# Gathering the tokens of two pairs of experts at once, and using three weight units in 24 unsplit instead of two, in a mixture-of-experts stage on one core

## The chip, the cores and the metric

The kernel runs on one core of one Trainium2 chip (trn2). The metric is device time in microseconds (us) from the start to the end of one launch. TensorE is written PE in the rows (PEld for its weight loads), VectorE is DVE, ScalarE is ACT, GpSimd is POOL, and SyncE (SP) issues nearly all DMA.

## What is computed

A one-layer transformer trunk in float32 over 256 tokens of width 2048: two token mixers (latent attention and retention), a gated merge, and then a hierarchical mixture of experts. The change touches the experts alone:

```python
def hier_moe(h, w_group, b_group, w_expert, b_expert, w1, w3, w2):
    ...
    g_sel = jnp.argmax(g_logits + b_group.astype(jnp.float32), axis=-1)
    ...
    _, e_local = lax.top_k(e_logits + e_bias, TOP_K)
    e_w = jax.nn.softmax(jnp.take_along_axis(e_logits, e_local, axis=-1), axis=-1) * g_prob[:, None]
    ...
    y = grouped_expert_ffn(xf, e_id, w1, w3, w2)
    out = jnp.einsum('nkd,nk->nd', y.reshape(n_tok, TOP_K, d), e_w.astype(y.dtype))
```

There are 32 experts, two are chosen for each token, and each expert is `(silu(x @ w1) * (x @ w3)) @ w2` with `w1` and `w3` of 2048 x 512 and `w2` of 512 x 2048.

## The kernel before

The first part of the launch (to about 1100 us) is the mixers. The change leaves it alone. Then comes the expert stage, which reads all 32 experts' weights once: 384 **units** of 1 MB, each a `[128, 2048]` tile of float32. An expert has 12 units, four each of `w1`, `w3` and `w2`. Experts are worked in 16 **pairs**, pair 0 to pair 15, with 24 units a pair. A unit has a place x in its pair from -4 to 19, and its step is k = x + 4. The steps of pair p are: k 0 to 3 `w1` of expert 2p, 4 to 7 `w2` of expert 2p-1, 8 to 11 `w3` of 2p, 12 to 15 `w1` of 2p+1, 16 to 19 `w2` of 2p, 20 to 23 `w3` of 2p+1. Pair 0 has no k 4 to 7, and four last `w2` units follow pair 15.

**One unit.** SyncE loads it into a ring of 8 slots (`raw2`; four early units have places of their own, `raw_e`). The load into a slot waits until TensorE is done with the unit that lay there 8 units before. ScalarE copies the unit to a rounded form (`hi`, line 636, tile `wh2`, 4 slots, so it waits until TensorE is done with the unit 4 before). VectorE subtracts it from the raw one (`lo`, line 786, written in place as `wl2`). TensorE then runs 8 matmuls of 512 columns, one on `wh2` and one on `wl2` for each quarter (lines 1119 and 1120). Such a unit is **split**. A unit that is **whole** (the places in `XR`, and the very first unit) is used by TensorE from the raw tile in plain float32 (line 1116) without work of ScalarE or VectorE: 4 matmuls in the program, shown by the trace as 8 of about 0.43 us.

**Gather.** Each expert has 64 slots for tokens. The tokens of a pair are gathered by TensorE: VectorE makes a 0/1 matrix `pg` (line 843), TensorE multiplies it with the token tiles `xh1` and `xl1` (the rounded part and the rest), 128 columns at a time (`gather`, line 1089, 8 calls of 8 matmuls a pair, one call behind each of the steps in `G_AT` = 4, 6, 8, 10, 16, 18, 20, 22 of the pair before), into PSUM banks 7 and 6 in turn. ScalarE copies each bank to `xg` (line 641). `xg` holds two pairs.

**Between.** `mix` (lines 1141 and 1144, 20 entries in the trace) transposes an expert's up-projections behind k 0 and k 12, into banks 6 and 7 too. Then come the sigmoid on ScalarE (653) and the product on VectorE (914 to 927, `hidden`). The outputs are scaled and added at k 7 and k 19 (ScalarE 660, VectorE 951). GpSimd scatters them to DRAM. In pair 15 ScalarE also copies the tokens of the second tile (line 707, steps 1 and 10), which the final sum takes. Each engine runs its instructions in the order written, and semaphores join the engines.

**The end.** Behind the last units SyncE reads the scattered rows back (`yrow`), TensorE adds the stream and the last pair, and VectorE normalises and the result goes out.

## Time and profile before

| | us |
|---|---|
| median of 3 runs | 2134.16 |
| lowest and highest | 2133.64, 2135.18 |
| span of the profiled execution | 2134.4 |
| TensorE busy | 2069.4 (97%) |
| TensorE weight loads | 1749.8 (82%) |
| VectorE busy | 1592.3 (75%) |
| ScalarE busy | 1286.2 (60%) |
| moved by DMA | 606.48 MB, 284 GB/s over the span |

The profiled execution is known by its span alone, from the first to the last instruction. Busy shares are averages over both parts of the launch, so the rows below are taken from the expert stage. Matmuls overlap in the trace, so the time of one is its start-to-start distance, not its listed duration.

### The profile page before, as it was taken

The page shows a single profiled execution, that of the slowest core. Times are in us where ns is not written, and L with a number is a line of the kernel's source. Part 1 is how long each engine was busy: PE and PEld are TensorE (multiplying, and loading weights), DVE is VectorE, ACT ScalarE, POOL GpSimd, SP SyncE. Part 2 cuts the span into 40 slices and gives each one's busy share as a digit, 9 for nine tenths or more (in the row PEclk, how much of TensorE's full clock was granted, in tenths as well). Part 3 has the DMA queues.
Part 4 walks back from the last instruction along what each step waited for, and adds up shares of the span by engine and source line. Part 5 has one row for each costly group of instructions (what it writes and reads, how often), then busy time and mean ns, then how long its engine had stood idle before and what let it go on. Part 6 is the DMA issues. An engine that isn't in the chain of part 4 may idle for free.

```text
span 2134.4 us, 30028 instructions
## 1 busy us (share of the span) xinstructions
PE 2069.4 (97%) x11452; PEld 1749.8 (82%) x11452; DVE 1592.3 (75%) x1450; ACT 1286.2 (60%) x1064; POOL 104.7 (5%) x76
## 2 busy tenths in 40 slices
PE   8999999999999999999999999999999999999986
PEld 8998888899999998887887777777777787777764
DVE  7646664453646375455669999999999999999988
ACT  5445653333333323334347888888888888888883
POOL 1000000000000000001000000000000000000010
PEclk9999999999999999999999999999999999999998
DMA  6554335655454544557777999999999999999996
GB/s 215 159 139 158 118 120 186 208 180 172 146 176 148 166 157 143 192 197 239 233 297 287 399 421 421 421 420 419 418 420 418 421 418 417 417 417 418 417 397 251
DMA packets 168608, 606.48 MB, mean 284 GB/s; under 512 B 20252, under 2 KB 32684, under 8 KB 117452
## 3 DMA queue, kind: packets, MB, share of 16 engines
q1 hardware_dynamic: 164976, 598.01, 73.9%
q0 software_dynamic: 3552, 7.37, 1.1%
q8 instruction: 55, 0.90, 0.2%
q14 instruction: 25, 0.20, 0.0%
HBM read 595.05 MB, written 22.04 MB: 289 GB/s over the span
## 4 chain that ended last, share of the span: by engine, by line
PE 64%; DVE 16%; issue 9%; DMA 7%; ACT 3%; DVEq 0%; POOLq 0%; POOL 0%; SPq 0%; ACTq 0%
PE ps L1991 19%; PE ps L1972 15%; DVE wl L786 11%; DMA raw<-in_w_dram 7%; PE ps L1119 5%; PE ps L1120 5%; PE ps L2349 4%; PE ps L1116 3%; ACT wh L636 2%; PE ps L2104 2%; PE ps L1141 1%; DVE yall L951 1%; PE ps L2064 1%; PE ps L1089 1%; PE ps L2077 1%
## 5 line engine op out<-in xcount | busy, mean ns | idle before, releaser
L786 DVE TENSOR_TENSOR wl<-raw,wh 128x2048 fp32r<-128x2048 f32 x347 | 780.9, 2288 | 39.7 <-ACT wh L636 38.4
L636 ACT ACTIVATE wh<-raw 128x2048 fp32r<-128x2048 f32 x347 | 661.6, 1915 | 132.8 <-DMA raw<-in_w_dram 72.6
L1548 DVE TENSOR_TENSOR wl<-raw,wh 128x2048 fp32r<-128x2048 f32 (+1 forms) x168 | 379.8, 2263 | 283.3 <-ACT wh L1350 283.3
L1350 ACT ACTIVATE wh<-raw 128x2048 fp32r<-128x2048 f32 (+1 forms) x168 | 317.9, 1895 | 444.6 <-DMA raw<-in_w_in_dram 264.7
L1119 PE MATMUL ps<-wh,xg 128*128 128x512 f32 x896 | 373.1, 416 | 25.0 <-DVE wl L786 24.5
L1120 PE MATMUL ps<-wl,xg 128*128 128x512 f32 x880 | 345.2, 392 | 0.0
L1972 PE MATMUL ps<-hth,wh 128*128 128x272 f32 (+1 forms) x896 | 259.8, 290 | 3.1 <-DVE wl L1548 1.8
L1972 PE MATMUL ps<-htl,wh 128*128 128x272 f32 (+1 forms) x896 | 255.7, 285 | 0.0
L1972 PE MATMUL ps<-hth,wl 128*128 128x272 f32 (+1 forms) x896 | 255.6, 285 | 0.0
L1119 PEld LDWEIGHTS ps<-wh,xg 128*128 128x128 f32 x896 | 169.1, 189 | 77.2 <-DVE wl L786 28.3
L1119 PE MATMUL ps<-wh,hx 128*128 128x512 f32 x508 | 202.4, 398 | 3.5 <-DVE wl L786 1.9
L1120 PE MATMUL ps<-wl,hx 128*128 128x512 f32 x508 | 198.6, 391 | 0.0
L1120 PEld LDWEIGHTS ps<-wl,xg 128*128 128x128 f32 x880 | 166.3, 189 | 37.8 <-issue 7.2
L1972 PEld LDWEIGHTS ps<-hth,wh 128*128 128x128 f32 x896 | 168.9, 188 | 5.8 <-DVE wl L1548 2.4
L1972 PEld LDWEIGHTS ps<-htl,wh 128*128 128x128 f32 x896 | 168.8, 188 | 0.3
L1972 PEld LDWEIGHTS ps<-hth,wl 128*128 128x128 f32 x896 | 168.6, 188 | 0.0
L1991 PE MATMUL ps<-wh,hth 128*128 128x512 f32 x384 | 156.1, 406 | 0.0
L1991 PE MATMUL ps<-wh,htl 128*128 128x512 f32 x384 | 151.3, 394 | 0.0
L1991 PE MATMUL ps<-wl,hth 128*128 128x512 f32 x384 | 150.8, 393 | 0.0
L1116 PE MATMUL ps<-raw,xg 128*128 128x512 f32 x256 | 115.1, 592 | 1.0 <-ACT xg L641 1.0
L1119 PEld LDWEIGHTS ps<-wh,hx 128*128 128x128 f32 x508 | 95.6, 188 | 24.1 <-issue 3.3
L597 POOL DMA_INDIRECT yscr<-yall,dest x30 | 67.6, 2255 | 887.5 <-DVE yall L951 887.5
(379 smaller groups left out, 3116.7 us busy)
## 6 DMA issues: line engine op xcount, KB each, us to landing
raw<-in_w_dram SPq DMA_DIRECT2D x380, 1024.0 KB, 10.4
raw<-in_w_in_dram SPq DMA_DIRECT2D x103, 1024.0 KB, 5.1
raw<-in_w_pa_dram SPq DMA_DIRECT2D x16, 1024.0 KB, 5.0
raw<-in_w_pb_dram SPq DMA_DIRECT2D x16, 1024.0 KB, 5.0
raw<-in_w_out_dram SPq DMA_DIRECT2D x16, 1024.0 KB, 5.1
raw<-in_w_ukv_dram SPq DMA_DIRECT2D x8, 1024.0 KB, 5.3
raw_e<-in_w_dram SPq DMA_DIRECT2D x4, 1024.0 KB, 8.1
yscr<-zeros SPq DMA_DIRECT2D x4, 1024.0 KB, 10.7
```

The lines of the kernel that those rows point to most:

```text
L597: pool.indirect_dma_start(yscr[:, :], bass.IndirectOffsetOnAxis(dest[0:SLOTS, par:par + 1], 0), yall[own_rows(par), :], None, bounds_check ...
L636: nc.scalar.activation(wh2[:, x % HELD, :], raw_of(turn, x), ACT.Copy).then_inc(s_wh2, 1)
L786: nc.vector.tensor_tensor(wl_of(turn, x), raw_of(turn, x), wh2[:, x % HELD, :].bitcast(F32), ALU.subtract).then_inc(s_wl2, 1)
L1116: m = nc.tensor.matmul(o, s.bitcast(F32), raw_of(turn, x)[:, c:c + 512], start=st, stop=sp_, skip_group_check=True)
L1119: nc.tensor.matmul(o, s, wh2[:, x % HELD, c:c + 512], start=st, stop=False, skip_group_check=True)
L1120: m = nc.tensor.matmul(o, s, wl_of(turn, x)[:, c:c + 512], start=False, stop=sp_, skip_group_check=True)
L1350: nc.scalar.activation(wh[:, n % RING1, 0:c], raw1[:, n % RING1, 0:c], ACT.Copy).then_inc(s_wh, 1)
L1548: nc.vector.tensor_tensor(wl[:, n % RING1, 0:c], raw1[:, n % RING1, 0:c], wh[:, n % RING1, 0:c].bitcast(F32), ALU.subtract).then_inc(s_wl, 1)
L1972: m = nc.tensor.matmul(ps[:, bank, col:col + width], w[:, n % RING1, c:c + P], s[:, 4 * u + k, c0:c0 + width], start=opens and u == 0 and ...
L1991: m = nc.tensor.matmul(ps[:, bank + t, :], s[:, 4 * u + k, c:c + P], w[:, n % RING1, 512 * k:512 * (k + 1)], start=u == 0 and k == 0 and j ...
L2104: m = nc.tensor.matmul(ps[:, bank + b, col:col + SEQ], w[:, n % RING1, c:c + P], s[:, k, X0:LT], start=opens and k == 0 and j == 0, stop=k ...
L2349: m = nc.tensor.matmul(ps[:, bank + t, :], s[:, 4 * u + k, P * t:P * (t + 1)], w[:, n % RING1, 512 * k:512 * (k + 1)], start=u == 0 and k ...
```

## The change

Three places in 24 are whole instead of two: x = 7 (step 11, the last `w3` unit of a pair's first expert) joins x = 10 and x = 22. Pairs 0 and 1 are gathered as before. From then on `gather_quad` gathers two pairs at once with 256 columns: 16 calls of 4 matmuls, one behind each of steps 3 to 10 and 15 to 22 of the odd pairs 1, 3, ..., 13. In the even pairs nothing is gathered. `xg` holds three pairs, some tiles move to other places, VectorE makes both matrices behind k 1 of the odd pairs, and the loops of TensorE, ScalarE and VectorE run over six pairs at a time. A `mix` waits also for the product before it (`s_hp`) and for the copies of the gathers (`s_xg`). At the end the load of the last normalisation's weights goes into a ring slot and waits for one more unit.

```diff
-        XR = (10, 22)
+        XR = (7, 10, 22)
...
-        xg = place("xg", [P, 2, KD, 2, 2 * SLOTS], 131072, F32R)
+        xg = place("xg", [P, 3, KD, 2, 2 * SLOTS], 131072, F32R)
...
-        G_AT = (4, 6, 8, 10, 16, 18, 20, 22)
+        G_QUAD = {**{3 + c: c for c in range(8)}, **{7 + c: c for c in range(8, KD)}}
+        CYCLE = 6
+        MATRICES = 2 + (PAIRS - 2) // 2
...
+        def quad_slots(n):
+
+            return sorted((n % 3, (n + 1) % 3))
+
+        def quad_next(n, last):
+
+            return n % 2 == 1 and not last
+
+        def cycles(eng, turn, pair):
+
+            with eng.Fori(0, (PAIRS - 4) // CYCLE) as i:
+                for m in range(CYCLE):
+                    pair(turn + 2 + CYCLE * i + m, CYCLE * i + 2 + m, 2 + m)
...
+                if isinstance(turn, int):
+                    done(sp, turn + PAIRS - 1, 20)
...
+            def gathered_quad(g, n, c):
+
+                act.wait_ge(s_gt, 8 * g + c + 1)
+                a, b = quad_slots(n)
+                nc.scalar.activation(xg[:, a:b + 1:b - a, c, :, :],
+                                     ps[:, 7 - c % 2, :].rearrange("p (i a c) -> p i a c", i=2, a=2),
+                                     ACT.Copy).then_inc(s_xg, 1)
...
+            def gather_matrix_quad(g, col, n):
+
+                need(dve, s_gt, 8 * g)
+                slots = slots2[:, :].rearrange("p (a s) -> p a s", a=2).unsqueeze(1).broadcast_to([P, TT, 2, SLOTS])
+                at = quad_slots(n)
+                for i in range(2):
+                    ranks = rk_[:, :, bass.ds(col + 2 * i, 2)].unsqueeze(3).broadcast_to([P, TT, 2, SLOTS])
+                    c = 2 * SLOTS * at.index((n + i) % 3)
+                    m = nc.vector.tensor_tensor(pg[:, :, c:c + 2 * SLOTS].rearrange("p t (a s) -> p t a s", a=2), slots,
+                                                ranks, ALU.is_equal)
+                m.then_inc(s_pg, 1)
...
-                    if k == 1 and not first and not last:
-                        gather_matrix(turn + 1, 2 * p + 2)
+                    if k == 1 and quad_next(n, last):
+                        gather_matrix_quad(turn + 1, 2 * p + 2, n + 1)
...
+            def gather_quad(g, c, matrix, products):
+
+                if c == 0:
+                    pe.wait_ge(s_pg, matrix)
+                need(pe, s_hp, products)
+                need(pe, s_xg, 8 * g + max(c - 1, 0))
+                bank = ps[:, 7 - c % 2, :].rearrange("p (e h s) -> p e h s", e=4, h=2)
+                for h, src in enumerate((xh1, xl1)):
+                    for t in range(TT):
+                        m = nc.tensor.matmul(bank[:, :, h, :], src[:, t, c, :],
+                                             pg[:, t, :].rearrange("p (e s) -> p e s", e=4),
+                                             start=t == 0, stop=t == 1, skip_group_check=True)
+                m.then_inc(s_gt, 1)
...
+                    elif quad and k < 4:
+                        pe.wait_ge(s_xg, 8 * turn + 4 * k + 4)
...
+                need(pe, s_hp, j)
...
-                        mix(turn - 1, j - 1, 1)
+                        mix(turn - 1, j - 1, 1, *([(s_xg, 8 * turn + KD)] if quad else []))
...
-                        mix(turn, j, 0, *([(s_hp, j), (s_stc, rounds)] if last else [(s_xg, 8 * (turn + 1) + 4)]))
+                        mix(turn, j, 0, *([(s_stc, rounds)] if last else [(s_xg, 8 * (turn + 1) + 4)] if first else
+                                          [(s_xg, 8 * (turn + 1) + 8)] if quad_next(n, last) else []))
...
+                    if k in G_QUAD and quad_next(n, last):
+                        c = G_QUAD[k]
+                        matrix = MATRICES * (rounds - 1) + p // 2 + 3
+                        gather_quad(turn + 1, c, matrix if cycle is None else matrix + CYCLE // 2 * cycle,
+                                    j if c < 8 else j + 1)
```

How the order moves. TensorE in pair 1, from one gather to the next. Before, eight gather matmuls of 2 x 64 columns stand behind step 4 and the next eight only behind step 6:

```order
L1089 MATMUL ps<-pg,xh_134 128x2x64 x2
L1089 MATMUL ps<-pg,xl_135 128x2x64 x2
L1089 MATMUL ps<-pg,xh_134 128x2x64 x2
L1089 MATMUL ps<-pg,xl_135 128x2x64 x2
L1119 MATMUL ps<-wh_125,hx 128x512
L1120 MATMUL ps<-wl_124,hx 128x512
L1119 MATMUL ps<-wh_125,hx 128x512
L1120 MATMUL ps<-wl_124,hx 128x512
```

Now, from behind step 3, there are four of 4 x 64 columns behind every step, with the eight matmuls of one unit between:

```order
L1126 MATMUL ps<-pg,xh_134 128x4x64 x2
L1126 MATMUL ps<-pg,xl_135 128x4x64 x2
L1171 MATMUL ps<-wh_125,hx 128x512
L1172 MATMUL ps<-wl_124,hx 128x512
L1171 MATMUL ps<-wh_125,hx 128x512
L1172 MATMUL ps<-wl_124,hx 128x512
L1171 MATMUL ps<-wh_125,hx 128x512
L1172 MATMUL ps<-wl_124,hx 128x512
L1171 MATMUL ps<-wh_125,hx 128x512
L1172 MATMUL ps<-wl_124,hx 128x512
L1126 MATMUL ps<-pg,xh_134 128x4x64 x2
L1126 MATMUL ps<-pg,xl_135 128x4x64 x2
```

The gather has moved to one call behind each of 16 steps in the odd pair, and none in the even one. The second place is TensorE in pair 0, unit 7, between the gather calls behind steps 10 and 11. Before (`raw_e`, `wl_e` are the early units' tiles):

```order
L1089 MATMUL ps<-pg,xh_134 128x2x64 x2
L1089 MATMUL ps<-pg,xl_135 128x2x64 x2
L1119 MATMUL ps<-wh_125,xg 128x512
L1120 MATMUL ps<-wl_e_133,xg 128x512
L1119 MATMUL ps<-wh_125,xg 128x512
L1120 MATMUL ps<-wl_e_133,xg 128x512
L1119 MATMUL ps<-wh_125,xg 128x512
L1120 MATMUL ps<-wl_e_133,xg 128x512
L1119 MATMUL ps<-wh_125,xg 128x512
L1120 MATMUL ps<-wl_e_133,xg 128x512
L1089 MATMUL ps<-pg,xh_134 128x2x64 x2
L1089 MATMUL ps<-pg,xl_135 128x2x64 x2
```

Now:

```order
L1141 MATMUL ps<-pg,xh_134 128x2x64 x2
L1141 MATMUL ps<-pg,xl_135 128x2x64 x2
L1168 MATMUL ps<-raw_e_129,xg 128x512 x4
L1141 MATMUL ps<-pg,xh_134 128x2x64 x2
L1141 MATMUL ps<-pg,xl_135 128x2x64 x2
```

The eight matmuls of the split unit have become four in plain float32. The third place is VectorE in pair 15, from the product behind k 0 to the one behind k 12. Before:

```order
L786 TENSOR_TENSOR wl_124<-raw_123,wh_125 128x2048 x4
L900 TENSOR_TENSOR pd<-slots_180,rk__167 128x512
L901 COPY wdc<-wd 128x8
L786 TENSOR_TENSOR wl_124<-raw_123,wh_125 128x2048 x3
L951 SCALAR_TENSOR_TENSOR yall<-ps,wsc,yall 64x2048
L786 TENSOR_TENSOR wl_124<-raw_123,wh_125 128x2048 x4
L914 TENSOR_TENSOR hv<-ps,sg 128x256
```

Now:

```order
L811 TENSOR_TENSOR wl_124<-raw_123,wh_125 128x2048 x4
L937 TENSOR_TENSOR pd<-slots_180,rk__167 128x512
L938 COPY wdc<-wd 128x8
L811 TENSOR_TENSOR wl_124<-raw_123,wh_125 128x2048 x2
L988 SCALAR_TENSOR_TENSOR yall<-ps,wsc,yall 64x2048
L811 TENSOR_TENSOR wl_124<-raw_123,wh_125 128x2048 x4
L951 TENSOR_TENSOR hv<-ps,sg 128x256
```

One subtraction (that of unit 7) is gone ahead of the output's sum, the `SCALAR_TENSOR_TENSOR`.

## Rows read from the trace of the kernel before

**Rows 1.** The page's slices: 40 equal slices of the span, about 53 us each.

```profile
GB/s 215 159 139 158 118 120 186 208 180 172 146 176 148 166 157 143 192 197 239 233 297 287 399 421 421 421 420 419 418 420 418 421 418 417 417 417 418 417 397 251
```

**Rows 2.** Windows: length, PE, PEld, DVE, ACT, POOL busy, PEclk, DMA share, GB/s.

```profile
1290.00:1970.00 680.00, 664.37 (x3322) 533.08 (x3320) 650.26 (x435) 582.88 (x427) 50.30 (x23) 1.00 1.01 419
```

**Rows 3.** Groups by line over five pairs of experts, 1395.56 to 1699.46 us.

```profile
L786 DVE TENSOR_TENSOR wl<-raw,wh 128x2048 fp32r<-128x2048 f32 x111 | 250.2, 2288 | 12.3 <-ACT wh L636 12.0
...
L636 ACT ACTIVATE wh<-raw 128x2048 fp32r<-128x2048 f32 x111 | 212.1, 1916 | 43.5 <-DMA raw<-in_w_dram 28.5 <-PE ps L1116 12.8 <-PE ps L1120 0.6
...
L1119 PE MATMUL ps<-wh,xg 128*128 128x512 f32 x280 | 116.5, 416 | 7.4 <-DVE wl L786 7.4
...
L641 ACT ACTIVATE xg<-ps 128x512 fp32r<-128x512 f32 x40 | 23.3, 583 | 0.1
```

**Rows 4.** Chain of waits in one pair: start, us, what (unit of work).

```profile
1517.36 1.73 PE ps L1141 x16
...
1521.46 3.43 PE ps L1116 x8
...
1528.54 0.84 PE ps L1089 x8
...
1530.13 0.23 PE ps L1120
...
1578.14 1.73 PE ps L1141 x16
```

**Rows 5.** SyncE's weight loads from 1400 to 1900 us, then 1220 to 1240.

```profile
L504 SPq DMA_DIRECT2D raw<-in_w_dram x198: 332/333/333, 1399.9 to 1897.7; - x198
...
DMA to landing us min/median/max: 8.7/10.5/12.2
...
L504 SPq DMA_DIRECT2D raw<-in_w_dram x9: 332/333/336, 1222.0 to 1239.4; - x9
...
DMA to landing us min/median/max: 7.9/9.2/10.9
```

**Rows 6.** TensorE timeline, 256-column matmuls: start, us, line, op, first and ninth.

```profile
99.72 0.28 PE L2077 MATMUL ps<-wh,ckh 128*128 128x256 f32 x1
...
100.67 0.28 PE L2077 MATMUL ps<-wh,ckl 128*128 128x256 f32 x1
```

**Rows 7.** Windows of 10 us at the stage's start, columns as in 2.

```profile
1140.00:1150.00 10.00, 10.00 (x61) 8.81 (x61) 9.79 (x14) 9.29 (x12) 0.00 (x0) 1.00 0.33 121
...
1190.00:1200.00 10.00, 10.00 (x49) 7.91 (x48) 9.15 (x6) 8.48 (x8) 0.00 (x0) 1.00 0.92 335
...
1220.00:1230.00 10.00, 10.00 (x45) 7.66 (x44) 8.69 (x5) 8.48 (x7) 0.00 (x0) 1.00 1.01 420
```

**Rows 8.** VectorE timeline at the first pair: start, us, line, op, count.

```profile
1161.57 15.50 DVE L786 TENSOR_TENSOR wl<-raw,wh 128x2048 fp32r<-128x2048 f32 x7
```

**Rows 9.** TensorE timeline, start of pair 1.

```profile
1181.92 0.47 PE L1119 MATMUL ps<-wh,xg 128*128 128x512 f32 x1 [1.72 <-DVE wl L786]
```

**Rows 10.** TensorE and VectorE timelines in the last pair.

```profile
2064.52 0.77 PE L1119 MATMUL ps<-wh,xg 128*128 128x512 f32 x1 [2.68 <-DVE wl L786]
...
2059.70 2.34 DVE L951 SCALAR_TENSOR_TENSOR yall<-ps,wsc,yall 64x2048 f32<-64x2048 f32 x1
...
2062.08 4.49 DVE L786 TENSOR_TENSOR wl<-raw,wh 128x2048 fp32r<-128x2048 f32 x2
```

**Rows 11.** Windows in the last pair: 2 and 10 us.

```profile
2064.00:2066.00 2.00, 1.48 (x4) 1.23 (x5) 2.00 (x2) 2.00 (x3) 1.14 (x1) 0.55 1.02 426
...
2070.00:2080.00 10.00, 10.00 (x39) 6.97 (x39) 8.54 (x10) 6.72 (x7) 1.34 (x1) 1.00 0.91 336
```

**Rows 12.** Last weight loads and their landing; ScalarE's conversion of the last unit.

```profile
L504 SPq DMA_DIRECT2D raw<-in_w_dram x3: 328/328/328, 2081.0 to 2084.6; - x3
...
DMA to landing us min/median/max: 8.1/8.8/9.4
...
2094.32 1.92 ACT L636 ACTIVATE wh<-raw 128x2048 fp32r<-128x2048 f32 x1 [1.72 <-PE ps L1120]
```

More of the change, by code:

```diff
@@ L673, in last_outputs, with pair @@
                                          ACT.Copy, scale=wsc[r, 1:2]).then_inc((s_yh, s_yc)[c], 1)
-            def pair(turn, par, first=False, early=None, last=False, rounds=None):
+            def pair(turn, p, n, first=False, early=None, last=False, rounds=None):
                 for x in body(first):
@@ L708, in pair @@
                                              (xh1, xl1)[k == 1][:, 1, :, :].bitcast(F32), ACT.Copy).then_inc(s_own, 1)
-                    for q in range(8):
-                        if k == (G_FIRST if first else G_AT)[q] and not last:
-                            gathered(turn + 1, 1 - par, q)
+                    if first and k in G_FIRST:
+                        gathered(turn + 1, n + 1, G_FIRST.index(k))
+                    if k in G_QUAD and quad_next(n, last):
+                        gathered_quad(turn + 1, n + 1, G_QUAD[k])
             def one_round(turn, rounds, early=None):
@@ L952, in output_rest, with pair @@
                                                ALU.add).then_inc(s_ye[par], 1)
-            def pair(turn, p, first=False, early=None, last=False):
+            def pair(turn, p, n, first=False, early=None, last=False):
                 for x in body(first):
@@ L984, in one_round @@
                         lo(turn, x)
-                pair(turn, 0, first=True, early=early)
+                pair(turn, 0, 0, first=True, early=early)
                 if early:
@@ L1146, in mix, with pair @@
                 m.then_inc(s_hm, 1)
-            def pair(turn, par, first=False, early=False, last=False, rounds=None):
+            def pair(turn, p, n, first=False, early=False, last=False, rounds=None, cycle=None):
+                quad = n % 2 == 0 and not first
                 for x in body(first):
```

99 lines of the change are left out of this document (50 added, 49 removed).

## The prediction

> **What bounds the kernel now.** I read the 40 slices first. The change lies in the expert stage, the last 19 slices or so, and there the reader sees DMA at 417 to 421 GB/s in every slice from 1227 us to 2028 us [rows 1]. The windows view over 1290 to 1970 us adds the DMA share, 1.01 of all 16 engines, and shows the other engines nearly as full: TensorE 664 of 680 us, VectorE 650, ScalarE 583 [rows 2]. So the busy shares don't say which of them sets the pace. Three things do.
>
> First, the groups by line: over five pairs (303.9 us) ScalarE waits 28.5 us for landings ahead of its conversions and TensorE 7.4 us for VectorE, that is 1.5 us a pair [rows 3]. So both ends of a unit's path wait for data now and then. Second, the pair lasts 60.78 us: a `mix` stands at 1517.36 and the same one of the next pair at 1578.14 [rows 4]. 24 units of 1.0486 MB in 60.78 us are 414 GB/s; the scatter and small transfers make up the 419. Third, a load takes 10.5 us from issue to landing (8.7 at least), over four times the 2.53 us in which one unit flows [rows 5]. There are always about four loads queued. Around 1220 to 1240 us the landing took only 7.9 to 10.9 us [rows 5] and the rate was the same 420 [rows 7]. So a later release of a slot costs nothing until the landing time falls below about 7.9 us. The steady pair is bound by DMA, and TensorE has 1.5 us a pair to spare.
>
> **The gather.** Eight gather matmuls of 128 columns take 0.84 us, 0.105 each [rows 4]. A pair has 64: 6.7 us. No matmul of the gather has 256 columns yet. The nearest rows are the 256-column matmuls of another stage with the same rounded operands: eight intervals in 0.95 us, 0.119 each [rows 6]. The bounds are 0.105 (as cheap as half the columns) and 0.21 (twice that); I take 0.119 since shape and operands are the same. 64 of them for two pairs are 7.6 us, all in the odd pair. So the odd pair pays 0.9 us more and the even one 6.7 us less. VectorE makes as many matrices as before, and ScalarE copies as many banks, 0.58 us each [rows 3], but 16 in the odd pair instead of 8: +4.7 us there, -4.7 us in the even one. Its idle time before conversions is 43.5 us in five pairs [rows 3], 8.7 us a pair, which covers this.
>
> **The third whole unit.** A split unit takes TensorE eight intervals of 0.23 us [rows 4], 1.86 us. A whole one takes 3.43 us [rows 4]: +1.57 us a pair. VectorE loses one subtraction of 2.29 us a pair and ScalarE one conversion of 1.92 us [rows 3].
>
> **The steady pairs.** TensorE needs 60.78 - 1.48 = 59.3 us a pair now. Afterwards an odd pair needs 59.3 + 1.57 + 0.9 = 61.8 us and an even one 59.3 + 1.57 - 6.7 = 54.2 us, 58.0 on the mean. That is 1.3 us less a pair, and DMA still needs 60.78. The odd pair falls 1.0 us behind and the even one makes it good; the queue covers it, because the landing time goes from 8.7 us at least to 7.7, beside the 7.9 that was seen to be harmless. ScalarE's longer second half of the odd pair may add as much again for a few steps. I count nothing for pairs 2 to 14, with bounds below. The new waits of `mix` for the copies and for the product are met some microseconds before (the last copies lie a step or two earlier, and the conversion that stood ahead of two of them, of a whole unit, isn't there), and behind `mix` stand units whose own data come later. Zero, and 0.3 us a pair as the upper bound.
>
> **The start.** Here DMA isn't the bound. Between 1140 and 1150 us it moves 121 GB/s while TensorE is busy all the time [rows 7]: the loads wait for slots that TensorE has not freed. Pair 0 gets the whole unit (step 11) and no cheaper gather. So its `mix` and all behind it come 1.57 us later. The lighter VectorE doesn't help: its seven subtractions start at 1161.57 behind the product of that `mix` [rows 8], and TensorE's wait of 1.72 us at 1181.92 is the end of that chain [rows 9]. Pair 1 adds 1.57 us (step 11) and 0.9 us (gather), of which about 0.8 us is a wait on VectorE that vanishes. DMA runs short until about 1200 (335 GB/s [rows 7]) and is full from then on. Pair 1's delay past 1.57 us reaches it only where the landing time was lowest, 7.9 us at about 1222. I take +0.8 us, with 0 and +2.5 as bounds. Together +2.4 us.
>
> **The end.** In pair 15 TensorE waits 2.68 us for VectorE at 2064.52, because ScalarE has two copies of the stream to make and VectorE's subtraction for that unit starts only at 2062.08, behind the sum at 2059.70 [rows 10]. Now VectorE has one subtraction less ahead of it, 2.29 us, and TensorE fills the gap with the whole unit, which waits for nobody. The matmuls behind the wait ran at a granted clock of 0.55 [rows 11], near the lower of the two levels (1.2 GHz), so the eight of step 12 took about 3.4 us instead of 1.86. By my count step 12 ends 3.2 us earlier relative to the loads: 2.68 of wait and about 1.6 of slow clock gone, less 1.57 for the whole unit, and 0.5 more as ScalarE and VectorE catch up. DMA had a hole there too: 336 GB/s for 10 us [rows 11] is 2.0 us lost, and I take it as gone. The last unit is bound by both sides. TensorE gives +2.4 - 3.2 = -0.8 us. Landing gives +2.4 - 2.0 = +0.4 us; it was at 2084.6 + 8.8 = 2093.4, and the conversion began at 2094.32 [rows 12], 0.9 later, which leaves -0.5 us. I take -0.6. The sums, scatter and normalisation behind it are the same, and the last normalisation's weights are loaded some 1 us later, 25 us before the end.
>
> **The sum.** 2134.4 (span) + 2.4 - 3.0 = 2133.8 us. The median of the runs is 0.24 us below the profiled span, so 2133.6 us.
>
> **A rule on the DMA rate.** The rows show 419 GB/s held over 680 us [rows 2]. The Trainium skill, in "DMA: Bandwidth & Descriptors", section "Where 436 GB/s comes from", says the fabric's ceiling is 435 GB/s, but that loads from HBM are held to about 358 GB/s a core. The trace disagrees with the 358: it shows 419. By the 435 the same pair would take an estimated 58.5 us, and the stage could gain up to 2.3 us a pair if something other than DMA held it back.
>
> **Rivals.**
>
> (a) DMA isn't quite at its limit, and relieved engines let it go faster. Slices within the stage lie between 417 and 421 [rows 1]. For it speaks that TensorE, VectorE and DMA are all within a few per cent of full [rows 2]. Against it speaks that the rate was the same at shorter queues [rows 5, 7]. At 421 instead of 419 over 800 us the gain is 4 us; at the 426 of a short window [rows 11] it is 13 us. I take 7: 2127 us.
>
> (b) The odd pairs starve the queue. It decides when TensorE's and ScalarE's lags together exceed what the queue covers, 8.7 - 7.9 = 0.8 us certainly and perhaps 2. TensorE lags 1.0, ScalarE's eight copies in a half pair are 2.3 us more than before. If 1.2 us of DMA is lost in each of the seven odd pairs, the time is 2133.6 + 8 = 2142 us. For it speaks the small margin; against it that ScalarE has 8.7 us of idle time a pair.
>
> (c) The 256-column matmuls with their strided moving and output tiles cost 0.21 us. An odd pair then needs 67.7 us, 6.9 over the pace; less some 2.5 in the queue, 4.4 are lost seven times: 2164 us. [Rows 6] speak against it.
>
> (d) TensorE's clock falls in the even pairs, where it now waits 6.6 us of 60.78. In this trace it fell behind a wait of 2.68 us [rows 10, 11], and not behind 1.72 us [rows 9]. The new idle time comes in pieces of 0.7 us, one a unit (2.53 less 1.86). Doubling eight matmuls in each of the 7 even pairs that follow would be 1.6 us each, mostly inside the slack: 2134 to 2140 us. The Trainium skill, "TensorE: Matmul & The Clock Gate", section "What's actually happening", says the slow clock is the default and only activity lifts it; the one fall here fits.
>
> (e) The change doesn't do what it says. The order shows the calls in place, so I give this nothing of its own.
>
> **How the numbers follow.** My forecast (DMA holds; between 2130 and 2138) has 0.66. (a) has 0.17, (b) 0.11, (c) 0.02, (d) 0.04, of which half within the bound. A measurement of this kernel can tell about 0.2% from no change, that is 4.3 us. That gives faster 0.17, same 0.68, slower 0.15. The range 2127 to 2141 leaves out half of (a), most of (b) and (c), a little under 0.2.
>
> **What the profile will show.** The pair's period 60.78 us, or two pairs 121.6, with DMA 419 GB/s and share 1.01. Gather calls of four matmuls in 0.48 us. TensorE busy about 52 to 54 of 60 us in even pairs and nearly all in odd ones. VectorE about 95 to 96% of what it was. Landing at least 7.5 us in odd pairs and up to 12 in even ones. Pair 1 begins at about 1183.5 instead of 1181.9. In pair 15 no wait of 2.7 us ahead of step 12 and no hole in DMA near 2075. I am wrong if the DMA rate rises with the lighter engines (a), or if it dips once in every odd pair (b).

## The result, and the profile after

The changed kernel takes 2146.1 us (median of 4 runs, 2144.4 to 2147.2) against 2134.6 us for the kernel before (2133.6 to 2135.2, 4 runs beside it). The ratio is 1.0054 with a 95% interval of 1.0041 to 1.0067: slower by some 11.5 us, and above the whole predicted range. The profiled execution took 2145.5 us, 2143.6 of them its span, against a span of 2134.4 before.

The page's slices of the changed kernel, to set against [rows 1]:

```profile
PEclk9999999999999999999999999999999999999998
...
GB/s 214 158 143 157 117 125 186 199 179 176 157 158 156 173 149 149 196 191 231 241 312 279 393 422 421 419 419 415 421 410 380 421 417 417 414 420 400 421 416 254
```

The expert stage is still at 417 to 421 GB/s in most slices, but not in all: 410 and 380 (1554 to 1661 us), 414, 400. The window of [rows 2] shows it as one number, 413 GB/s for 419 (columns as there), and the windows below it hold the largest hole. The last three are around the place of [rows 11]:

```profile
1290.00:1970.00 680.00, 648.50 (x2914) 490.29 (x2913) 617.21 (x420) 545.47 (x410) 49.54 (x22) 0.99 1.01 413
1610.00:1620.00 10.00, 5.92 (x25) 4.74 (x23) 5.71 (x3) 5.21 (x6) 1.99 (x1) 0.83 0.95 377
1620.00:1630.00 10.00, 10.00 (x45) 7.15 (x45) 7.48 (x9) 6.10 (x5) 0.00 (x0) 1.00 0.79 278
1630.00:1640.00 10.00, 9.32 (x41) 7.37 (x40) 10.00 (x7) 9.95 (x7) 0.00 (x0) 1.00 0.98 384
...
2060.00:2070.00 10.00, 8.75 (x35) 6.07 (x35) 9.97 (x8) 9.71 (x7) 0.00 (x0) 1.00 1.00 419
2070.00:2080.00 10.00, 10.00 (x47) 7.32 (x48) 8.27 (x4) 9.99 (x7) 2.26 (x1) 1.00 1.02 426
2080.00:2090.00 10.00, 10.00 (x38) 6.91 (x38) 9.81 (x11) 7.51 (x7) 1.53 (x1) 1.00 1.01 415
```

Three things are new on TensorE, and one on ScalarE. First its timeline at 1615 us (start, us, line and shape; in brackets the idle time before it and what ended it), then ScalarE's at the same place:

```profile
1615.51 0.49 PE L1171 MATMUL ps<-wh,xg 128*128 128x512 f32 x1 [4.08 <-issue]
1615.84 0.39 PE L1172 MATMUL ps<-wl,xg 128*128 128x512 f32 x1
1616.07 0.41 PE L1171 MATMUL ps<-wh,xg 128*128 128x512 f32 x1
1616.30 0.60 PE L1172 MATMUL ps<-wl,xg 128*128 128x512 f32 x1
...
1617.98 0.63 PE L1172 MATMUL ps<-wl,xg 128*128 128x512 f32 x1
```

```profile
1611.96 1.90 ACT L654 ACTIVATE wh<-raw 128x2048 fp32r<-128x2048 f32 x1
1618.64 1.91 ACT L654 ACTIVATE wh<-raw 128x2048 fp32r<-128x2048 f32 x1 [4.79 <-PE ps L1172]
```

Pair 8 begins here, and with it the second turn of the loops of six pairs. TensorE stands still for 4.08 us with no releaser ("issue"). ScalarE's 4.79 us end at 1618.64 us, just behind TensorE's last matmul on the unit of step 0 (the 1617.98 row), whose slot this conversion needs. So this row alone doesn't show a stop of ScalarE's own; the runs without TensorE's jump do. The kernel before jumps back five times on TensorE and shows no such wait. In the page's third part the queues that carry instructions have grown, from 55 and 25 packets before to

```profile
q8 instruction: 78, 1.28, 0.2%
q14 instruction: 39, 0.32, 0.0%
```

(packets, MB, share). Then TensorE ahead of the first unit of an odd pair, and ahead of the first gather call of an odd pair:

```profile
1425.41 0.79 PE L1171 MATMUL ps<-wh,xg 128*128 128x512 f32 x1 [2.60 <-DVE wl L811]
1426.00 0.63 PE L1172 MATMUL ps<-wl,xg 128*128 128x512 f32 x1
```

```profile
1315.96 0.50 PE L1126 MATMUL ps<-pg,xh 128*128 128x256 f32 x2 [0.89 <-DVE pg L879]
```

The wait of 2.6 to 2.7 us comes at the end of each of the seven even pairs, and behind five of them the matmuls run at the slow clock at first (0.63 us in place of 0.39). The wait for the gather's matrix was not there before: the first gather call then stood at step 4, now at step 3. In the changed kernel it stands in pairs 3 and 9 alone (0.89 and 0.66 us), the two odd pairs whose first matmuls were not slow.

Last, the landing of SyncE's loads, in the odd pair's dip of 1590 to 1600 us (385 GB/s), for [rows 5]:

```profile
L520 SPq DMA_DIRECT2D raw<-in_w_dram x8: 332/333/333, 1581.5 to 1599.7; - x8
...
DMA to landing us min/median/max: 6.7/7.7/9.3
```

**Where the 9.2 us of span lie.** The `mix` at step 0 of pair 3 starts at 1304.27 us before and at 1305.55 after: +1.3 at the start. The one of pair 15 starts at 2033.61 and 2046.27: the twelve pairs between take 729.3 and 740.7 us, +11.4. From there to the end of the span it is 100.8 and 97.3 us: -3.5. So start and end came out near the forecast, and all of the loss is in the steady pairs, which I had counted at nothing.

### The profile page after: what moved, and what is told of

The parts are those of the page before. It is cut to its first block, busy times and chain, and to the rows that moved or that the text cites. A ratio compares the mean times of both kernels' runs of the same rounds, so it can differ in the third digit from the quotient of the medians.

```text
span 2143.6 us, 28967 instructions
## 1 busy us (share of the span) xinstructions
PE 2064.3 (96%) x11004; PEld 1705.4 (80%) x11004; DVE 1559.3 (73%) x1434; ACT 1248.7 (58%) x1048; POOL 104.8 (5%) x76
## 4 chain that ended last, share of the span: by engine, by line
PE 75%; DVE 9%; issue 6%; DMA 6%; ACT 4%; POOLq 0%; DVEq 0%; POOL 0%; ACTq 0%; SPq 0%
PE ps L2054 19%; PE ps L2035 15%; PE ps L1171 8%; PE ps L1172 7%; PE ps L1168 7%; DMA raw<-in_w_dram 5%; DVE wl L811 5%; PE ps L2412 4%; PE ps L1194 2%; ACT wh L654 2%; PE ps L1126 2%; PE ps L2167 2%; PE ps L2127 1%; PE ps L2140 1%; DVE wl L1611 1%
## 5 line engine op out<-in xcount | busy, mean ns | idle before, releaser
L811 DVE TENSOR_TENSOR wl<-raw,wh 128x2048 fp32r<-128x2048 f32 x332 | 749.1, 2288 | 78.9 <-ACT wh L654 75.8
L654 ACT ACTIVATE wh<-raw 128x2048 fp32r<-128x2048 f32 x332 | 630.1, 1915 | 143.8 <-PE ps L1172 52.5
L1171 PE MATMUL ps<-wh,xg 128*128 128x512 f32 x832 | 358.3, 431 | 37.4 <-DVE wl L811 31.9
L1172 PE MATMUL ps<-wl,xg 128*128 128x512 f32 x820 | 326.6, 398 | 0.0
L1171 PEld LDWEIGHTS ps<-wh,xg 128*128 128x128 f32 x832 | 159.1, 191 | 99.1 <-DVE wl L811 48.6
L1172 PEld LDWEIGHTS ps<-wl,xg 128*128 128x128 f32 x820 | 157.3, 192 | 38.8 <-issue 10.8
L1168 PE MATMUL ps<-raw,xg 128*128 128x512 f32 x376 | 169.1, 592 | 1.0 <-ACT xg L667 1.0
L1168 PEld LDWEIGHTS ps<-raw,xg 128*128 128x128 f32 x376 | 70.7, 189 | 71.9 <-issue 67.5
```

The source lines that it names most:

```text
L654: nc.scalar.activation(wh2[:, x % HELD, :], raw_of(turn, x), ACT.Copy).then_inc(s_wh2, 1)
L811: nc.vector.tensor_tensor(wl_of(turn, x), raw_of(turn, x), wh2[:, x % HELD, :].bitcast(F32), ALU.subtract).then_inc(s_wl2, 1)
L1168: m = nc.tensor.matmul(o, s.bitcast(F32), raw_of(turn, x)[:, c:c + 512], start=st, stop=sp_, skip_group_check=True)
L1171: nc.tensor.matmul(o, s, wh2[:, x % HELD, c:c + 512], start=st, stop=False, skip_group_check=True)
L1172: m = nc.tensor.matmul(o, s, wl_of(turn, x)[:, c:c + 512], start=False, stop=sp_, skip_group_check=True)
```

## The experiments

Each was run against the kernel before (median 2134.7 to 2135.4 us beside them). Where the text compares two experiments, it is by their medians. The first four looked at the parts.

**pe_straight.** TensorE's loop of six pairs written out, so that it doesn't jump back:

```diff
-                with pe.Fori(0, (PAIRS - 4) // CYCLE) as i:
-                    for m in range(CYCLE):
-                        pair(turn + 2 + CYCLE * i + m, 2 + m, 2 + m, rounds=rounds, cycle=i)
+                    for n in range(2, PAIRS - 2):
+                        pair(turn + n, 2 + (n - 2) % CYCLE, n, rounds=rounds, cycle=(n - 2) // CYCLE)
```

> The changed kernel with TensorE's loop of six pairs (run twice) written out as straight code; ScalarE's and VectorE's loops stay. In the changed kernel TensorE stood still for 4.1 us at 1611.4 us, where the second turn of that loop begins, and the two-pair interval that holds it is 127.2 us instead of 121.6. Theory 'jump back' (TensorE has to fetch the code of a long loop body again): the wait of 4.1 us is gone and the kernel is 4 to 5.5 us faster than the changed one, some 2141 us. Rival 'clock and unevenness' (the loss is that of uneven pairs alone): no gain, 2145 to 2147 us. A second rival, that long straight code costs fetches of its own, would show as several waits with no releaser along the stage and a time at or above the changed kernel's.

2144.5 us, 1.6 less; the runs (2142.2 to 2146.0 us) overlap the changed kernel's. The 4.08 us wait is gone, and the 2.7 us waits stay. The hole wasn't the whole loss, nor did taking it away give back its own 4 us.

**whole_alone and quad_alone.** The two parts apart, first on the kernel before, then on the changed one:

```diff
-        XR = (10, 22)
+        XR = (7, 10, 22)
```

```diff
-        XR = (7, 10, 22)
+        XR = (10, 22)
```

> The kernel before with three whole units in 24 and its own gather and loops. TensorE then needs 59.3 + 1.57 = 60.9 us a pair against the 60.8 of the loads. Theory (the whole unit costs nothing in the steady pairs): start +1.6, end -2 to -3, so 2133 to 2136 us. Rival (TensorE becomes the bound, with its own short waits on top): up to 0.5 us a pair over 13 pairs, 2138 to 2142 us.

> The changed kernel with two whole units in 24, as before: the gather of two pairs alone. Theory 'the wait of 2.6 us at the end of an even pair drops TensorE's clock, and the uneven pairs and the jump back do the harm': all of the steady loss stays, the start is 1.6 us better and the end up to 3 us worse than in the changed kernel, so 2144 to 2150 us. Rival 'the third whole unit does the harm' (TensorE's 61.8 us in the odd pair over the 60.8 of the loads): 2138 to 2140 us, with only the jump back's 4 us left.

The third whole unit alone takes 2135.9 us, ratio 1.0001 (0.9992 to 1.0011): nothing. The gather alone, with its loops, takes 2168.2 us (2152 to 2181): far worse than either theory said. TensorE there waits 2.6 us not once but twice in two pairs, and its granted clock is 0.94 on the mean of 1300 to 1660 us. The trace is that of the slowest of its four runs, 2181 us:

```profile
1399.80 0.52 PE L1171 MATMUL ps<-wh,xg 128*128 128x512 f32 x1 [2.59 <-DVE wl L811]
1431.08 0.80 PE L1171 MATMUL ps<-wh,xg 128*128 128x512 f32 x1 [2.58 <-DVE wl L811]
...
1300.00:1660.00 360.00, 338.41 (x1485) 259.95 (x1484) 325.12 (x219) 287.10 (x216) 24.78 (x11) 0.94 0.98 397
```

The additional wait (1399.80) stands ahead of step 12 of the even pair. In the changed kernel the whole unit of step 11 fills that time, and the wait and the slow matmuls behind it are gone.

**warm.** Ten matmuls of 128 columns that nobody reads, in a free part of a bank, fill the 2.7 us wait:

```diff
+                    if k == 23 and n % 2 == 0 and n and not last:
+                        for _ in range(10):
+                            nc.tensor.matmul(ps[:, 7, 2 * P:3 * P], ones[:, :], ident[:, :], start=True, stop=True,
+                                             skip_group_check=True)
```

> The changed kernel with ten idle matmuls of 128 columns (ones with the identity, into a part of PSUM bank 7 that nobody reads) behind step 23 of the even pairs 2 to 14, about 2.2 us of TensorE work where it waited 2.6 us for VectorE. Theory 'clock': the granted clock stays at 1.00 there and each of the four or five pairs that began at about 0.57 gives back some 1.4 us, so 2139 to 2142 us. Rival (the clock's fall costs nothing since DMA is the bound, or the added work costs what it saves): 2145 to 2148 us.

2144.4 us, 1.7 less (2143.5 to 2146.9 us, so these runs overlap the changed kernel's too). **straight_warm** joins it with pe_straight.

> The changed kernel with both earlier remedies: TensorE's loop of six pairs written out, and ten short matmuls behind the last unit of each even pair that fill the 2.7 us wait. The jump back took 4.1 us of TensorE (a hole in DMA of some 5 us by the windows from 1610 to 1640 us), the matmuls alone gave 1.7 us. If the two are independent they add: 2141 to 2143 us, no wait of TensorE over 1.8 us left between 1190 and 2040 us, and dips of DMA that remain only some 50 us into each odd pair. If one hides the other, it stays at the 2144.5 us of the written-out loop alone.

2141.6 us, as expected: 4.5 less than the changed kernel, and every run (2140.9 to 2142.7) is below all of the changed kernel's and all of warm's. No wait of TensorE over 1.7 us is left between 1190 and 2040 us, and 6.5 us are still missing against the kernel before.

**half_products, half_copies, early_matrix_all, early_half, early_matrix** looked for them in the odd pairs. half_products and half_copies are straight_warm with half of the gather's matmuls or of its copies:

```diff
-                    for t in range(TT):
+                    for t in range(1):
```

```diff
-                nc.scalar.activation(xg[:, a:b + 1:b - a, c, :, :],
...
+                w = 2 * SLOTS if n == 2 else SLOTS
+                nc.scalar.activation(xg[:, a:b + 1:b - a, c, :, 0:w],
```

early_matrix_all (on straight_warm), early_half (on half_products) and early_matrix (on the changed kernel) move VectorE's matrix half a pair ahead:

```diff
-                    if k == 1 and quad_next(n, last):
-                        gather_matrix_quad(turn + 1, 2 * p + 2, n + 1)
+                    if k == 1 and n == 1:
+                        gather_matrix_quad(turn + 1, 2 * p + 2, n + 1)
+                    if k == 15 and n % 2 == 0 and 0 < n < PAIRS - 2:
+                        gather_matrix_quad(turn + 2, 2 * p + 4, n + 2)
```

> As straight_warm, but each two-pair gather call leaves out its second token tile (two matmuls instead of four, so wrong tokens are gathered; ScalarE's copies and VectorE's matrices stay). It takes about 3.8 us of TensorE out of each odd pair and nothing of ScalarE. Theory, TensorE's surplus in odd pairs (61.8 us of work for 60.8 us of loads) starves the queue: the dips of DMA 40 to 50 us into each odd pair vanish and the time is 2133 to 2137 us. Rival, ScalarE's eight more copies in the second half of an odd pair do it: the dips stay and the time is within 1.5 us of straight_warm.

> As straight_warm, but each of ScalarE's copies of the two-pair gather takes only the upper halves (256 of 512 columns) from the second such gather on, so the lower halves of the gathered tokens are stale. TensorE's work stays. It takes some 0.2 us from each of 16 copies, about 3 to 4 us of ScalarE, out of each odd pair. Theory (TensorE's surplus): dips stay, time within 1.5 us of straight_warm. Rival (ScalarE's copies): dips vanish and the time is 2133 to 2137 us.

> straight_warm, and VectorE makes the matrix of the two-pair gather half a pair earlier: behind step 15 of the even pair before, instead of behind step 1 of the odd pair. In straight_warm TensorE waits for it 0.75 to 0.8 us ahead of the first gather call (step 3) of the odd pairs, and runs 0.9 us later for it; the first half of an odd pair took 32.4 us there, where its matmuls need some 31.4. Theory: this wait, on top of the 0.9 us of dearer products, is what starves the queue; without it the first half takes 31.4 to 31.6 us, the two-pair period 121.6 to 122 us instead of 122.6, and the time is 2136 to 2138 us. Rival (the surplus of products, or the fetching of instructions by the long loops): the period stays and the time is within 1.5 us of straight_warm's 2141.6.

> half_products (which leaves out the second token tile of each gather call) with the early matrix. half_products still had waits of 0.76 us for the matrix, and 2.0 us for ScalarE's copy at the last gather calls. If the waits of TensorE in the odd pairs are what counts, and not its products, this is as fast as early_matrix_all within 1.5 us; if the surplus of products is a cause of its own, it is 2 to 3 us faster than that, 2133 to 2135 us.

> The changed kernel with that one edit alone: the matrix half a pair earlier, loop of six pairs on TensorE and no extra matmuls. The jump back (4 us) and the slow clock behind the 2.7 us waits stay. Theory: 3 to 5 us less than the changed kernel, 2141 to 2143 us. Rival: 2146 us, no change.

They took 2140.7, 2142.7, 2142.1, 2141.3 and 2147.1 us. The first four lie within 1.1 us of straight_warm, and the fifth is 1.0 above the changed kernel. Wherever a theory named a part of the odd pair as the cause and forecast a gain, none came. The edits did what they should: in early_matrix_all the first half of an odd pair took 31.3 us (1306.13 to 1337.44) for 32.4 in straight_warm, and the smallest landing time from 1700 to 1720 us rose from 7.7 to 8.7 us. The kernel was no faster. In half_products a new wait shows part of how:

```profile
1359.18 0.35 PE L1126 MATMUL ps<-pg,xh 128*128 128x256 f32 x1 [2.04 <-ACT xg L660]
```

**long_loop_before and single_gather** turned to the loops. The first is the kernel before with TensorE's loop of two pairs made one of six (the diff). The second has everything but the gather: the third whole unit, TensorE's pairs written out, and ScalarE's and VectorE's loops six pairs long.

```diff
-                with pe.Fori(1, PAIRS // 2 - 1) as i:
-                    pair(turn + 2 * i, 0)
-                    pair(turn + 2 * i + 1, 1)
+                with pe.Fori(0, (PAIRS - 4) // 6) as i:
+                    for m in range(6):
+                        pair(turn + 2 + 6 * i + m, m % 2)
```

> The kernel before with TensorE's loop of two pairs, run six times, turned into a loop of six pairs run twice; nothing else changes. If the length of the loop's body is what makes the jump back wait, TensorE waits some 4 us at about 1614 us without a releaser, DMA has a hole of 3 to 5 us behind it, and the time is 2138 to 2140 us. If the wait in the changed kernel came from something else (the new waits, the matrix counter), the time stays within 1 us of the kernel before.

> The kernel before with the third whole unit, TensorE's pairs written out and ScalarE's and VectorE's loops made six pairs long as in the changed kernel: all of the change but the two-pair gather, and no jump back on TensorE. Instructions are then fetched throughout the expert stage as in the changed kernel. If this fetching costs anything, the time is 2138 to 2141 us; if only the gather does, it is whole_alone's 2135.9 us within 1 us.

long_loop_before: 2139.3 us, +4.1, with this row in it:

```profile
1610.37 0.49 PE L1119 MATMUL ps<-wh,xg 128*128 128x512 f32 x1 [4.04 <-issue]
```

So the jump back alone stops TensorE, with no other edit in the kernel. The 4.1 us can't all be put down to the stop, though. The runs scatter (2135.5 to 2145.3 us), and in the profiled one 2.6 us are lost ahead of the jump, in pairs 5 and 6 (124.2 us for 121.6). There TensorE waits for VectorE, and the matmuls behind are slow:

```profile
1515.06 0.72 PE L1119 MATMUL ps<-wh,xg 128*128 128x512 f32 x1 [1.85 <-DVE wl L786]
1515.58 0.63 PE L1120 MATMUL ps<-wl,xg 128*128 128x512 f32 x1
```

ScalarE, whose loop is short in this run, stands still behind the jump too, for the slot that TensorE has not freed:

```profile
1613.88 1.91 ACT L636 ACTIVATE wh<-raw 128x2048 fp32r<-128x2048 f32 x1 [5.03 <-PE ps L1120]
```

single_gather: 2141.1 us. Without any two-pair gather the kernel is as slow as straight_warm, so what the two have in common, the third whole unit and the long code, came under suspicion.

**whole_straight, long_others, straight_before, extra_copies** divided that up. The first has only TensorE's pairs written out (on whole_alone), the second only ScalarE's and VectorE's loops made six pairs long (on whole_alone), the third is the first without the third whole unit, and the fourth has 29 extra transfers (last diff).

```diff
-                with act.Fori(1, PAIRS // 2 - 1) as i:
-                    pair(turn + 2 * i, 0)
-                    pair(turn + 2 * i + 1, 1)
+                with act.Fori(0, (PAIRS - 4) // 6) as i:
+                    for m in range(6):
+                        pair(turn + 2 + 6 * i + m, m % 2)
...
-                with dve.Fori(1, PAIRS - 1) as p:
-                    pair(turn + p, p)
+                with dve.Fori(0, (PAIRS - 4) // 6) as i:
+                    for m in range(6):
+                        pair(turn + 2 + 6 * i + m, 6 * i + 2 + m)
```

```diff
+                sp.dma_start(dscr[bass.ds(e, 1), :],
+                             w2[bass.ds(e, 1), 0:2, :].rearrange("a p n -> a (p n)")).then_inc(s_extra, 16)
```

> whole_alone with TensorE's pairs written out and nothing else: the loops of ScalarE and VectorE stay short. TensorE's instructions (the 16 KB packets of the instruction queue) are then fetched all through the expert stage, and there is no jump back. single_gather took 2141.1 us with all three engines' code long, whole_alone 2135.9 with all short. If TensorE's packets do it (29 of 16 KB, against 18 of 8 KB of the other queue), 2139 to 2141 us; if the other engines' packets do, 2136 to 2137 us.

> whole_alone with ScalarE's and VectorE's loops made six pairs long, and TensorE's loop of two pairs kept. The counterpart of whole_straight: if TensorE's packets cost the time, 2136 to 2137.5 us; if the others' do, 2139 to 2141 us. The two runs' losses should add up to some 5 us.

> The kernel before (two whole units) with TensorE's pairs written out and nothing else. If the fetching costs the same whatever TensorE has to spare, it loses as much against before as whole_straight does against whole_alone, 3 to 5 us: 2138 to 2140 us. If it costs only because TensorE has no time to spare with three whole units, it is under 1 us: 2135 to 2136 us.

> whole_alone with 29 extra transfers of 16 KB (two rows of the experts' weights into an unused place in HBM, two a pair, nobody waits for them), as large and as many as the instruction packets that the long loops add; no loop changes. If such a packet costs by taking one DMA engine for about a microsecond while each unit's landing waits for all 16 engines, the time is 2138 to 2141 us. If it costs by what the fetching does elsewhere (in the engine's own sequencer), the time is whole_alone's within 1 us, since 0.5 MB at 420 GB/s is 1.1 us.

2135.6, 2142.2, 2135.6 and 2137.0 us. Long code on TensorE without a jump costs nothing that shows, with two or three whole units. Long loops on ScalarE and VectorE cost 6.3 us over whole_alone. extra_copies is 1.1 us above whole_alone, which is what its bytes take and also within the spread of the runs (2135.2 to 2138.0); each of its transfers went out as some 32 small packets and not as one of 16 KB, so it doesn't copy an instruction packet, and says nothing on those. ScalarE at the place of the second turn in long_others, and then in whole_straight:

```profile
1608.83 1.92 ACT L636 ACTIVATE wh<-raw 128x2048 fp32r<-128x2048 f32 x1 [0.40 <-DMA raw<-in_w_dram]
1614.52 1.91 ACT L636 ACTIVATE wh<-raw 128x2048 fp32r<-128x2048 f32 x1 [3.78 <-PE ps L1123]
```

```profile
1609.18 1.91 ACT L636 ACTIVATE wh<-raw 128x2048 fp32r<-128x2048 f32 x1 [0.69 <-DMA raw<-in_w_dram]
1611.75 1.91 ACT L636 ACTIVATE wh<-raw 128x2048 fp32r<-128x2048 f32 x1 [0.66 <-DMA raw<-in_w_dram]
```

**scalar_straight and all_straight** wrote out ScalarE's pairs on top of straight_warm, and then VectorE's too:

```diff
-                cycles(act, turn, pair)
+                    for n in range(2, PAIRS - 2):
+                        pair(turn + n, n, 2 + (n - 2) % CYCLE)
```

> straight_warm (2141.6 us) with ScalarE's pairs written out as well; only VectorE keeps its loop of six pairs. In every run with ScalarE's long loop, and in none with its short one, ScalarE stands still 3.0 to 5.5 us at about 1611 to 1618 us, where its second turn begins, with nothing of its own to wait for, and the time lies 5 to 6 us above the same kernel with a short loop (long_others 2142.2 against 2135.9). Theory, ScalarE's jump back is the cause, once, and TensorE with no time to spare never makes it good: the idle time at 1611 is gone and the time is 2135 to 2138 us. Rival, VectorE's loop or the small instruction packets: it stays within 1.5 us of 2141.6.

> scalar_straight with VectorE's pairs written out too, so no engine but SyncE jumps back in the expert stage; the two-pair gather, the third whole unit and the short filling matmuls stay. If VectorE's jump back costs anything of its own, it is 1 us or more faster than scalar_straight; by the theory it is the same within 1 us, 2135 to 2138 us. Either way it gives the price of the two-pair gather itself, against whole_straight's 2135.6.

scalar_straight stayed at 2141.3 us: the theory that named ScalarE alone fell. Its first premise was wrong as well: ScalarE stands still with a short loop too, 5.03 us in long_loop_before, and the waits of 4.6 to 5.5 us all belong to runs in which TensorE jumps. ScalarE's own stop is read where TensorE has no long loop: 3.0 to 3.9 us in eight runs. In scalar_straight that wait is gone, and behind it stands VectorE's own, at the same place:

```profile
1612.51 2.29 DVE L815 TENSOR_TENSOR wl<-raw,wh 128x2048 fp32r<-128x2048 f32 x1 [0.57 <-ACT wh L654]
1618.37 2.29 DVE L815 TENSOR_TENSOR wl<-raw,wh 128x2048 fp32r<-128x2048 f32 x1 [3.56 <-ACT wh L654]
```

With both gone it is 2139.1 us (2137.7 to 2139.7, all below scalar_straight's). The three engines' stops overlap, so that taking away one uncovers the next.

**Two-pair periods.** Each is the time from the `mix` of step 0 of an odd pair to that of the next odd pair, in us, from the `mix` rows of each trace. The jump back falls in the third.

| kernel | 3-5 | 5-7 | 7-9 | 9-11 | 11-13 | 13-15 |
|---|---|---|---|---|---|---|
| before | 121.6 | 121.6 | 121.6 | 121.3 | 121.7 | 121.6 |
| whole_straight | 121.4 | 121.4 | 122.0 | 121.5 | 121.5 | 121.5 |
| long_loop_before | 120.7 | 124.2 | 125.7 | 120.1 | 120.7 | 121.9 |
| long_others | 121.3 | 121.7 | 124.0 | 122.0 | 122.8 | 122.3 |
| single_gather | 121.5 | 121.8 | 123.7 | 122.0 | 122.8 | 122.1 |
| changed | 123.3 | 122.9 | 125.7 | 122.8 | 123.3 | 122.7 |
| straight_warm | 122.1 | 123.0 | 124.0 | 121.8 | 122.3 | 122.7 |
| all_straight | 121.7 | 122.3 | 122.6 | 122.3 | 122.2 | 122.4 |

Up to the jump, long_others is as fast as whole_straight (243.1 and 242.9 us), though it fetches code all the time. So it is the jump that costs, not the fetching. Behind it the periods stay 0.5 to 1.3 us longer, and DMA dips (305 GB/s from 1650 to 1655 us). In long_loop_before, with two whole units, the two periods behind the jump are instead 1.2 and 1.0 us shorter than in the kernel before. That fits a TensorE that with three whole units has no time left to catch up, but long loops of ScalarE and VectorE with two whole units were not run, so this reason is not shown. all_straight has no jump and still needs 0.3 to 0.9 us more in each period than whole_straight. That part is the gather's, with the filling matmuls. In four of the six odd pairs from 3 to 13 DMA dips about 40 us in (400, 399, 360 and 369 GB/s over 10 us), and the loads land in as little as 7.1 us. The third dip in all_straight, and then the same place in whole_straight:

```profile
1710.00:1720.00 10.00, 10.00 (x46) 7.58 (x45) 9.16 (x11) 8.48 (x8) 0.00 (x0) 1.00 0.97 360
...
DMA to landing us min/median/max: 7.2/7.9/9.6
```

```profile
1710.00:1720.00 10.00, 10.00 (x54) 8.52 (x53) 9.40 (x5) 10.00 (x8) 0.00 (x0) 1.00 0.99 401
...
DMA to landing us min/median/max: 7.9/8.4/9.9
```

**The whole loss as a chain of measured steps** (medians, each with its neighbour):

| step | us | difference |
|---|---|---|
| before | 2135.1 | |
| third whole unit, TensorE's pairs written out (whole_straight) | 2135.6 | +0.5 |
| the two-pair gather, with the filling matmuls (all_straight) | 2139.1 | +3.4 |
| jumps back of ScalarE and VectorE (straight_warm) | 2141.6 | +2.5 |
| jump back of TensorE (warm) | 2144.4 | +2.8 |
| the 2.7 us waits and the slow clock (changed) | 2146.1 | +1.7 |

The first and the last difference lie within the spread of the runs; at the other three no two runs of neighbours overlap. The steps don't add up in every order: TensorE's long loop alone costs 4.1 us in the kernel before, and taking it from the changed kernel alone gains 1.6.

## Why the prediction was wrong

**The steady pairs at zero: wrong by 11.4 us.** This is the step that failed: "I count nothing for pairs 2 to 14", with 0.3 us a pair as the upper bound, where the twelve pairs measured lost 0.95 us each. It failed in four ways.

*The loops' length was not in the sum.* The diff says `CYCLE = 6` and three engines' loops grow by it; I costed the work in a pair, and nothing for the code around it. The jumps back cost 5.3 us in the chain above. The Trainium skill, "Advanced Engine Details and Errata", section "ISA Cache", gives the store for instructions as 32 KB an engine and 128 KB on TensorE, and I hadn't weighed it. By the two instruction queues the trace agrees. These are their rows over twelve pairs, 1303 to 2033 us of the kernel before and then 1303 to 2043 us of the changed one; that q8 is TensorE's and q14 the other two's follows from whole_straight (29 and 2 packets) and long_others (5 and 18):

```profile
q8 instruction: 5, 0.08, 0.0%
q14 instruction: 2, 0.02, 0.0%
```

```profile
q8 instruction: 28, 0.46, 0.2%
q14 instruction: 18, 0.15, 0.0%
```

*Rival (d) was taken lightly for a wrong reason.* I wrote that the new idle time comes in pieces of 0.7 us. It does within the even pair, but at its end 2.6 to 2.7 us come in one piece: VectorE makes the output's sum there (2.35 us), ahead of the subtraction that TensorE waits for. [Rows 10] show that very pattern in pair 15, and I read it as a thing of the last pair. Its price by the chain was 1.7 us in all, within what I gave it and within the spread of the runs; that it would happen at all I gave 0.04.

*A landing time of 7.9 us "seen to be harmless" was read from one window of nine loads [rows 5, 7].* I took it as the queue's margin, and the smallest landing time turned out to be none. Dips stand at minima of 6.7 to 7.2 us, but also at 8.3 us (half_products, 362 GB/s from 1740 to 1750 us) and at 9.0 us (whole_straight, 387 GB/s from 1770 to 1780 us). I had forecast 7.7 in the odd pairs, and it went to 6.7 in pair 7 (1590 us). TensorE doesn't wait for the matrix in that pair; what stands ahead is the 2.59 us wait and the slow matmuls. Where the wait for the matrix does come in every odd pair but one at 0.74 to 0.78 us, in straight_warm, taking it away lifted the landing times and not the speed. I had counted VectorE's matrices and not where the first call stands: step 3 in place of step 4.

*Rival (b), a dip of DMA in the odd pairs, came in part.* I priced it at 1.2 us an odd pair, 8 us in all; all_straight shows 0.3 to 0.9 a period, 3.4 us in all, with a dip in four odd pairs. Its mechanism, lags of TensorE and ScalarE that exceed what the queue covers, is not shown: halving the gather's matmuls or its copies gained 0.9 us and lost 1.1.

**What held.** The gather calls take 0.46 to 0.48 us for four matmuls of 256 columns, as forecast from [rows 6], which does away with rival (c). The third whole unit costs nothing and gives nothing in the kernel before (whole_alone). Pair 1 begins at 1183.30 us with a wait of 1.62 (forecast 1183.5; before [rows 9]):

```profile
1183.30 0.47 PE L1171 MATMUL ps<-wh,xg 128*128 128x512 f32 x1 [1.62 <-DVE wl L811]
```

The start lost 1.3 us by pair 3 where I had 2.4. By the `mix` rows it was 1.4 us at pair 1 (1183.83 to 1185.23) and 2.7 at pair 2 (1244.05 to 1246.77), so pair 1 did cost more, and pair 2, which gathers nothing, made 1.4 us of it good. At the end the wait of [rows 10] and the hole of [rows 11] are gone: 415 to 426 GB/s from 2060 to 2090 us, and 3.5 us gained where I had 3.0. Rival (a), a faster DMA, is not seen: no slice is above 422. On the Trainium skill's 358 GB/s a core for loads from HBM ("DMA: Bandwidth & Descriptors", "Where 436 GB/s comes from") the runs say what [rows 2] said: whole_alone moves 419 GB/s on the mean of 1303 to 2033 us. The measurement decides.

**What stays open.** What makes up the gather's 3.4 us: the dearer odd pair, the matrix's wait, or the filling matmuls, which all_straight has and whole_straight has not. What lowers the DMA rate in the dips is open too. half_products, half_copies and early_matrix_all were made with ScalarE's and VectorE's jumps still in them. They show that none of the three alone brings the time back there, and can't divide what is left without the jumps. Nor was the changed kernel run with all loops written out and without the filling matmuls.

## What to carry to other kernels

When a change makes a loop's body longer, count it on every engine: look for a wait with no releaser where each engine's second turn begins, and compare the instruction queues' packets before and after. Before an idle time is put down to the engine's own jump, look whether what it needs was there: in the changed kernel ScalarE's 4.79 us ended with TensorE's work. Stalls that stand side by side on several engines hide each other, so one experiment that removes one of them and gains nothing doesn't acquit it. And when a pipeline is bound by one resource with another just behind it, don't count two periods of unequal work at their mean: here they cost 3.4 us where the mean forecast nothing, and one window's landing time was no measure of the margin.

## What the runs showed of the hardware

- A jump back into a loop of six pairs stops TensorE for 4.0 to 4.3 us (five runs), ScalarE for 3.0 to 3.9 (the eight runs in which TensorE doesn't make such a jump) and VectorE for 3.6 (scalar_straight). The kernel before, with loops of one or two pairs, shows no such wait where it jumps back.
- Code that is fetched straight on costs nothing measurable: whole_straight and straight_before take 2135.6 us, 0.5 above the kernel before.
- Behind a wait of 2.6 to 2.7 us TensorE's granted clock fell to the lower level (1.2 GHz; 0.53 from 1425 to 1428 us) in most cases and not in all: not at 1303 and 1675 us in the changed kernel, where what went before was the same to the eye. It also fell behind a wait of 1.85 us in long_loop_before (0.83 from 1514 to 1524 us), and not behind the 1.72 us of [rows 9]. Seven of the ten filling matmuls stand in the trace and take 0.94 us together; with them in the wait the clock stayed at full speed (straight_warm's mean is 0.996, as before).
- A stop of some 3 to 4 us each on two engines off the bound, once in a launch, cost 5 to 6 us in single_gather and long_others: the periods behind it stay longer.
- Ten-microsecond windows of low DMA rate (360 to 400 GB/s) came with smallest landing times from 6.7 (the changed kernel, 385 GB/s from 1590 us) up to 9.0 us (whole_straight, 387 GB/s from 1770 us), so that time alone doesn't tell whether the queue suffices.
